# A hybrid encoder block: the seam from the first feed-forward to the mixer, and the two norms at w_out, in a new order

## The reference, cut to what matters

```python
x = x + 0.5 * swiglu(rms_norm(x, ff1_norm), ff1_w_gate, ff1_w_up, ff1_w_down)
proj = rms_norm(x, mix_norm) @ w_in                  # q | k | v | u
attn = banded_sink_attention(q, k, v, sink)          # (1024, 512)
ssm = s5_ssm_glu(u, ..., w_glu, b_glu)               # z * sigmoid(z @ w_glu + b_glu), (1024, 512)
mixed = concat(rms_norm(attn, attn_out_norm), rms_norm(ssm, ssm_out_norm))
x = x + mixed @ w_out                                # (1024, 1024)
x = x + 0.5 * swiglu(rms_norm(x, ff2_norm), ff2_w_gate, ff2_w_up, ff2_w_down)
out = rms_norm(x, final_norm)
```

## Time and profile before

| | |
|---|---|
| median of 3 runs | 1717.98 us (1716.14 to 1724.11) |
| profiled execution | 1726.49 us, span 1724.8 us, mean clock of PE 0.972 |
| PE busy | 1654.2 us, 96% |
| DVE, ACT, POOL busy | 1089.9 (63%), 726.0 (42%), 555.6 (32%) |
| longest single wait of PE | 9.05 us, before the sum at 653.84 |

### The profile page before, as it was taken

How to read it: one execution, slowest core, us unless ns; L and a number is a source line. 1 busy time by engine, 2 the same in 40 slices (tenths; PEclk the granted TensorE clock), 3 DMA queues, 4 the chain that set the end, 5 groups by cost and what they waited for, 6 DMA issues and landing times.

```text
span 1724.8 us, 21900 instructions
## 1 busy us (share of the span) xinstructions
PE 1654.2 (96%) x7540; PEld 1356.4 (79%) x7540; DVE 1089.9 (63%) x1691; ACT 726.0 (42%) x1321; POOL 555.6 (32%) x974
## 2 busy tenths in 40 slices
PE   7999999999999997999798799999999999999998
PEld 5778888888888876887576588878888888888886
DVE  5966667766778856313854536866656665667755
ACT  6444443344344435313356534444433334444443
POOL 4005788877677865100432433000000000000012
PEclk8999999999999998999788899999999999999998
DMA  6354433343795541415732025132342233685443
GB/s 210 123 91 103 135 137 125 112 136 140 249 323 169 137 133 41 157 49 105 97 67 68 25 76 175 67 98 98 102 142 99 98 115 124 228 309 164 123 110 116
DMA packets 156246, 223.23 MB, mean 129 GB/s; under 512 B 17904, under 2 KB 96368, under 8 KB 152944
## 3 DMA queue, kind: packets, MB, share of 16 engines
q1 hardware_dynamic: 153072, 214.27, 40.3%
q0 software_dynamic: 3072, 7.62, 2.3%
HBM read 151.90 MB, written 69.96 MB: 129 GB/s over the span
## 4 chain that ended last, share of the span: by engine, by line
PE 55%; POOL 24%; issue 6%; DMA 5%; DVE 5%; ACT 3%; POOLq 1%; SPq 1%; DVEq 0%; ACTq 0%
PE bank L1031 17%; PE bank L1032 16%; PE bank L1033 16%; POOL EBb L2847 2%; POOL ptmp L2846 2%; POOL ptmp L2845 2%; POOL pw L2660 2%; POOL ssq L2561 2%; POOL EBb L2861 2%; POOL ptmp L2860 2%; POOL ptmp L2859 2%; DMA cs_scratch<-EBb 1%; POOL ptmp L2806 1%; POOL ptmp L2804 1%; POOL cl_st L2810 1%
## 5 line engine op out<-in xcount | busy, mean ns | idle before, releaser
L1031 PE MATMUL bank<-hbhi,ws_lo 128*128 128x512 f32 x1056 | 414.0, 392 | 9.0 <-DVE ws_lo L2019 4.9
L1032 PE MATMUL bank<-hblo,ws_hi 128*128 128x512 f32 x1056 | 411.9, 390 | 0.0
L1033 PE MATMUL bank<-hbhi,ws_hi 128*128 128x512 f32 x1056 | 411.8, 390 | 0.0
L2561 POOL TENSOR_TENSOR ssq<-ssq,sqt 128x512 f32<-128x512 f32 x54 | 77.6, 1436 | 736.2 <-ACT sqt L1494 732.2
L1031 PE MATMUL bank<-d_hi,ws_lo 128*128 128x512 f32 x616 | 242.3, 393 | 2.2 <-DVE d_lo L2189 2.2
L1031 PEld LDWEIGHTS bank<-hbhi,ws_lo 128*128 128x128 f32 x1056 | 198.7, 188 | 56.3 <-issue 6.8
L1032 PE MATMUL bank<-d_lo,ws_hi 128*128 128x512 f32 x616 | 241.0, 391 | 0.0
L1033 PE MATMUL bank<-d_hi,ws_hi 128*128 128x512 f32 x616 | 240.9, 391 | 0.0
L1033 PEld LDWEIGHTS bank<-hbhi,ws_hi 128*128 128x128 f32 x1056 | 198.8, 188 | 41.7
L1032 PEld LDWEIGHTS bank<-hblo,ws_hi 128*128 128x128 f32 x1056 | 198.8, 188 | 41.0 <-issue 0.5
L1562 ACT ACTIVATE loc<-bank 128x512 f32<-128x512 f32 x160 | 95.6, 597 | 254.9 <-PE bank L1033 254.9
(11 more groups left out here) (273 smaller groups left out, 2656.2 us busy)
## 6 DMA issues: line engine op xcount, KB each, us to landing
b_scratch<-loc SPq DMA_DIRECT2D x42, 1024.0 KB, 7.2
d_in<-b_scratch SPq DMA_DIRECT2D x154, 256.0 KB, 3.1
raw2a<-in_ff_w_up_dram SPq DMA_DIRECT2D x44, 512.0 KB, 4.7
loc<-in_ff_w_gate_dram SPq DMA_DIRECT2D x36, 512.0 KB, 4.7
x_scratch<-xT SPq DMA_DIRECT2D x4, 2048.0 KB, 10.9
dw_lo_place<-in_ff_w_down_dram SPq DMA_DIRECT2D x8, 1024.0 KB, 7.8
xT<-x_scratch SPq DMA_DIRECT2D x8, 1024.0 KB, 6.5
x_in<-in_x_dram SPq DMA_DIRECT2D x8, 512.0 KB, 7.0
```

What stands on the lines that cost most here:

```text
L1031: nc.tensor.matmul(o, wl, rh, start=first, stop=False, skip_group_check=chain)
L1032: nc.tensor.matmul(o, wh, rl, start=False, stop=False, skip_group_check=chain)
L1033: return nc.tensor.matmul(o, wh, rh, start=False, stop=last, skip_group_check=chain)
L2561: pool.tensor_tensor(ssq[:, hs(h)], ssq[:, hs(h)], sqt[:, a % 2, :], ALU.add).then_inc(ssq_done, 1)
```

## The change

- **Seam.** `N_TAIL` is 2. Squares 0 to 3 of half 0 (tiles complete after product 1) are made on ACT before the splits of steps 40, 41, 42 and 46, and DVE adds them (`early_add`); POOL keeps four additions of half 0. For N_MIX, `ssq` and `sqt` lie in `dw_hi_place`, so ACT's wait for the landing moves behind the scalings of half 0, and POOL waits for a landing at the start of the next round. ACT's squares 4 to 9 alternate with the splits of steps 70 to 72; the Newton step of half 0 moves ahead of split 73 on DVE. The spread comes after step j = 4.
- **The end** gets the same early squares and `N_TAIL`.
- **w_out.** Halves 1 of N_ATT and N_SSM get bank 3, their own root and Newton buffers and their own diagonal; the state-space squares get `ssq_y`, `sqt_y` and semaphores of their own and go with the gates, in the order tile by tile, half 0 and half 1. Both attention sums stand behind gate 3, both spreads behind gate 5. First parts go in the order 0 to 5, both state-space sums after part 1, both spreads after part 3. Then channel tile 4 of all six blocks, tile 5 of all six, and tiles 6 and 7 block by block. Gate product 3 uses bank 4.

```diff
-N_TAIL = 3
+N_TAIL = 2
+EARLY_SQUARES = {40: 0, 41: 1, 42: 2, 46: 3}
+EARLY_ADDS = {40: 1, 41: 2, 44: 3}
...
-         + [("S", N_ATT, 6), ("S", N_ATT, 7), ("G", 2), ("R", N_ATT, 0), ("G", 3), ("G", 4)]
+         + [("S", N_ATT, 6), ("S", N_ATT, 7), ("G", 2), ("S", N_SSM, 0), ("G", 3), ("R", N_ATT, 0), ("R", N_ATT, 1)]
...
+GLU_BANK = [0, 1, 2, 4]
-SPREAD_BANK = {(N_FF2, 1): 6, (N_END, 1): 0}
+SPREAD_BANK = {(N_ATT, 1): 3, (N_SSM, 1): 3, (N_FF2, 1): 6, (N_END, 1): 0}
...
+    if norm == N_SSM:
+        return i % 2, i // 2
...
-                elif (what, n) == ("step", 5):
+                elif (what, n) == ("step", 4):
                     norm_spread(norm, 0)
...
-                    wait_lo(pe, split_before(N_FF2))
+                    wait_lo(pe, split_before(N_SSM) + 2 * (k - 3))
...
         for o in range(8):
             glu(o)
-            if o == 2 or o == 6:
-                norm_sum(N_ATT, o // 6)
-            elif o == 4 or o == 7:
-                norm_spread(N_ATT, o // 7)
-
-        pe.wait_ge(o_taken, 8)
-        out_part(0, range(4))
-        norm_sum(N_SSM, 0)
-        out_part(1, range(4))
-        norm_spread(N_SSM, 0)
-        out_part(3, range(4))
-        norm_sum(N_SSM, 1)
-        out_part(4, range(4))
-        norm_spread(N_SSM, 1)
-        out_part(2, range(4))
-        out_part(5, range(4))
+            if o == 3:
+                norm_sum(N_ATT, 0)
+                norm_sum(N_ATT, 1)
+            elif o == 5:
+                norm_spread(N_ATT, 0)
+                norm_spread(N_ATT, 1)
+
+        for i in range(6):
+            out_part(i, range(4))
+            if i == 1:
+                norm_sum(N_SSM, 0)
+                norm_sum(N_SSM, 1)
+            elif i == 3:
+                norm_spread(N_SSM, 0)
+                norm_spread(N_SSM, 1)
+        for k in (4, 5):
+            for i in range(6):
+                out_part(i, (k,))
...
-                out_part(i, range(4, KD)).then_inc(mix_out, 1)
+                out_part(i, (6, 7)).then_inc(mix_out, 1)
...
+            pool.wait_ge(eb_stored, i * 32 + 16)
...
-            pool.wait_ge(eb_stored, i * 32 + 32)
```

More of the change, by code:

```diff
@@ L87, in squares_before @@
 def squares_before(norm):
-    return sum(2 * t for t in NORM_TILES[1:norm])
+    return sum(2 * NORM_TILES[n] for n in range(1, norm) if n != N_SSM)
 def adds_before(norm):
-    return sum(2 * (t - 1) for t in NORM_TILES[1:norm])
+    return sum(2 * (NORM_TILES[n] - 1) for n in range(1, norm) if n != N_SSM)
 def sums_before(norm):
@@ L547, in htmp, with dgt, ssq_of, sqt_of @@
         return htmps[norm >= N_ATT][:, c % HTMP, :]
-    def dgt(norm):
-        return dgts[norm]
+    def dgt(norm, h):
+        return dgts[(N_ATT, N_SSM)[h]] if norm in (N_ATT, N_SSM) else dgts[norm]
+    def ssq_of(norm, h):
+        if norm == N_SSM:
+            return ssq_y[:, hs(h)]
+        return dw_hi_place[:, h, HALF:] if norm == N_MIX else ssq[:, hs(h)]
+    def sqt_of(norm, a):
+        return dw_hi_place[:, 2 + a % 2, HALF:] if norm == N_MIX else sqt[:, a % 2, :]
     def spread_bank(norm, h):
@@ L1038, in norm_sum @@
             last = max(i for i in range(2 * kt) if half_and_tile(norm, i)[0] == h)
-            pe.wait_ge(ssq_done, add_number(norm, last) + 1)
+            if norm == N_SSM:
+                pe.wait_ge(ssq_y_done, 6)
+            else:
+                pe.wait_ge(ssq_done, add_number(norm, last) + 1)
             if norm in NORMED:
-                before = split_before(norm) + h * kt
+                before = {(N_MIX, 1): KD, (N_ATT, 0): split_before(N_ATT), (N_SSM, 0): split_before(N_ATT) + 4,
+                          (N_SSM, 1): split_before(N_SSM)}.get((norm, h))
                 if before:
@@ L1487, in square @@
                     act.wait_ge(sum_ready, sums_before(norm))
-                dst = ssq[:, hs(h)]
+                dst = ssq_of(norm, h)
             else:
@@ L1688, in ffn @@
                 down_b(w, q)
-            down_split(w, range(N_SLOT, 70))
+            for q in range(N_SLOT, 70):
+                if q in EARLY_SQUARES:
+                    if (w, q) == (0, 40):
+                        act.wait_ge(t_stored, 16 * N_PAIR)
+                    down_square(w, EARLY_SQUARES[q])
+                down_split(w, (q,))
         def x_squares(h):
@@ L1877, in _ @@
             else:
-                h, k = at_[1] // 4, at_[1] % 4
-                act.wait_ge(glu_done, 2 * k + h + 1)
-                square(*at_, yT[:, k, hs(h)])
+                i = at_[1]
+                h, k = scale_order(N_SSM, i)
+                act.wait_ge(glu_done, i + 1)
+                if i >= 4:
+                    act.wait_ge(ssq_y_done, i - 3)
+                act.activation(ssq_y[:, hs(h)] if i < 2 else sqt_y[:, i % 2, :], yT[:, k, hs(h)], ACT.Square
+                               ).then_inc(sq_y_done, 1)
         def mix_src(i):
@@ L1914, in _ @@
         ffn(1)
-        for i in range(8):
-            down_square(1, i)
-        down_split(1, (70, 71, 72))
-        for i in range(8, 12):
-            down_square(1, i)
+        down_square(1, 4)
+        down_square(1, 5)
+        down_split(1, (70,))
+        down_square(1, 6)
+        down_square(1, 7)
+        down_split(1, (71,))
+        down_square(1, 8)
+        down_square(1, 9)
+        down_split(1, (72,))
         norm_std(N_END, 0)
+        down_square(1, 10)
+        down_square(1, 11)
         down_split(1, range(73, N_DSTEP))
@@ L2340, in _ @@
         ffn(0)
-        for q in range(70, 74):
+        for q in range(70, 73):
             down_split(0, q)
+        norm_rms(N_MIX, 0)
+        down_split(0, 73)
         split_lo(U_IN, U_IN + 1)
-        norm_rms(N_MIX, 0)
         down_split(0, 74)
@@ L2533, in out_rows @@
                 ins.then_inc(fin_taken, 1)
-        for q in range(70, 74):
+        for q in range(70, 73):
             down_split(1, q)
         norm_rms(N_END, 0)
+        down_split(1, 73)
         for t in range(3):
@@ L2554, in add_square @@
             h, k = half_and_tile(norm, n)
-            if begins(norm, n):
+            if begins(norm, n) or norm in (N_MIX, N_END) and n < 4:
                 return
@@ L2916, in _, with add_square_y @@
             pool.tensor_copy(mark[:, :], unit[:, 0, 0, :]).then_inc(state_done, 1)
+        def add_square_y(i):
+            if i < 2:
+                return
+            h, k = scale_order(N_SSM, i)
+            pool.wait_ge(sq_y_done, i + 1)
+            if i >= 4:
+                pool.wait_ge(ssq_y_done, i - 3)
+            pool.tensor_tensor(ssq_y[:, hs(h)], ssq_y[:, hs(h)], sqt_y[:, i % 2, :], ALU.add).then_inc(ssq_y_done, 1)
         for kind, *at_ in GATED:
-            if kind == "S":
+            if kind == "S" and at_[0] == N_SSM:
+                add_square_y(at_[1])
+            elif kind == "S":
                 add_square(*at_)
```

122 lines of the change are left out of this document (76 added, 46 removed).

## The result

The changed kernel takes 1709.28 us (median of 7 executions, 1707.12 to 1710.87), the kernel before 1724.11 (7 executions, 1716.14 to 1728.04): a ratio of 0.9919, interval 0.9899 to 0.994. So it is faster, by some 14 us, and clear of noise. 1699.0 was forecast with a range up to 1708, so the forecast is wrong: the kernel lies 1.3 us above the range. Two numbers already disagree. The profiled executions differ by 18.5 us (spans 1724.8 and 1706.3), close to the forecast's 19.0; the medians differ by 14.8. And the kernel before spreads over 12 us, the changed one over 4. The three executions of before that stand ahead of the prediction (median 1717.98) are three of these seven.

What follows compares the result with a forecast made beforehand. PE, busy 96% of the span, was taken as the bound, so only its waits and slow-clock stretches could be won: 14.8 (seam) + 2.5 (w_out) + 1.7 (end) = 19.0 off 1718.0 gave 1699.0 us, range 1692 to 1708.

Steps and rivals of the forecast that it cites:

- the Sum: Whole kernel: gains of 14.8, 2.5 and 1.7 make 19.0 us, taken off the median of 1718.0, giving 1699.0.
- the seam's lower bound of 9: Seam to the mixer: least gain, 9 us, if POOL still waits for its landing (642.6) and the sum comes at 649.4.
- The prediction's own signs of being wrong: Changed profile: PE doesn't wait for `ssq_y` at w_out, or the seam still shows more than 2 us idle.
- The seam, 14.8: First feed-forward to mixer: no PE wait at the sum or on `d_lo`; 14.8 us gained, bounds 9 and 15.3.
- W_out, 2.5: Norms at w_out: old waits go, new ones of 3.3, 1.1, 8.2 and 4.0 come; 2.5 us gained net.
- Contention, 0.3: W_out: DVE's subtractions stretched while POOL adds, charged 0.3 us since POOL is mostly idle then.
- The end, 1.7: Before the last product: 3.0 us gained, POOL's last addition 1.3 later; 1.7 net, between 0 and 3.
- (a): W_out: the hand-offs of ACT and DVE are quicker, gain 10.7 there, time 1690.8 us; chance 0.10.
- (b): W_out: 17 hand-offs are slower by 0.4 each or contend, 6.8 us in all, time 1705.8; chance 0.14.
- (c): Seam: POOL still held by its landing, sum waits 4.6 us, slow matmuls (3) stay, time 1706.6; chance 0.05.
- (d): W_out's merged sum makes it slower: w_out takes 105 us, the whole 1719; chance 0.03.
- (e): Steps 40 to 46: early squares on ACT hold up loads and PE, 2 us; chance 0.04.

Runs made afterwards that it cites:

- after_again: The changed kernel run once more with no edit, beside the kernel before: 1709.85 us, ratio to before 0.9933.
- w2_early: Against the changed kernel, the split of w_out's third unit (unit 2) put ahead of the two state-space roots: 1704.85 us, ratio to before 0.9916.

## Why the prediction was wrong

**The step that failed is the base, in the Sum:** "what changes is waits, so I take it off the median". Of the 10.3 us between 1699.0 and 1709.28, 6.1 are the base and 4.2 the terms taken off it. The base, 1717.98, was the median of three executions; with four more, run beside the changed kernel, the median of before is 1724.11, and over the 27 of after_again's group 1722.47. The terms were read from one execution of 1726.5, 8.5 above that base, and the forecast never asked what the 8.5 were. The runs show a good part of it: the wait of 9 us is itself a thing that some executions have and others don't. Of the four profiles that have the seam as before, two (times 1726.5 and 1725.4) show it and two (1716.7 and 1714.7) show one of 2.6 or 2.7. To take the whole wait off a time that may not hold it counts it twice. Whether the executions of 1716.1 and 1718.0 were of the early kind is inferred from their times; they have no profiles.

Against the profiled early execution (span 1713.0) the change is worth 6.7 us and not 19.0: 6.6 up to the wait on `qT`, and the rest cancels. Against the late one it is worth 18.5, and that looks like the forecast's 19.0, but this is partly luck. The three terms measured 13.4, 0.5 and 1.6, in sum 15.5; the mixer's 2.6, in good part chance of the clock, and 0.5 ahead of the seam fill the gap.

The range failed for the same reason: the seam's lower bound of 9 was thought out for the changed kernel (POOL still held), while the one that came true lay on the side of the kernel before (the wait mostly not there). Both hints stood in what I had: the earlier trace rows show ACT released by a DMA, and three times of one kernel spread over 8 us. The prediction's own signs of being wrong couldn't show it either: all of them are rows of the changed kernel, and nearly all came as named.

**The seam, 14.8.** 13.4 in the profiled pair (38.3 to 24.9). No wait at the sum, as forecast. Of the missing 1.4, about 0.9 is the wait of 1.16 on DVE's take of output 0, which the forecast had put 0.2 behind PE: DVE does two splits of w_in's units first (2.36 us, until 668.5). The six steps behind the spread take 16.9, or 2.82 each and not 2.72; most of that is the first matmul behind the spread. Against an early execution of before the term is 6.6, as above.

**W_out, 2.5.** The waits are right, each within 0.8 and in sum 16.9 against 17.0 with the last of 0.5. The gain is 0.5 in the profiles and nothing in the medians. The term that was mis-sized is the slow matmuls: PE was to be busy 68.0 of 85.0 and is so 70 of 87. Two sums in one piece took 3.6 for the 2.7 forecast, two spreads behind them 1.3 for 1.1, and after the 8 us wait PE's granted clock was 0.63 over 16.1 us. PE's idle time went up from 13.7 to 17.2 us, 3.3 of it for the split of unit 2, which the new order didn't need to put behind the roots (w2_early).

**Contention, 0.3.** DVE's subtraction beside POOL's additions of squares took 1.09 at 946.25 and the split of unit 1 took 1.47 for 1.23: about 0.4 and 0.2, so twice the charge and still small. The Trainium skill (GPSIMD Engine Reference, Specifications) says that GpSimd contends for SBUF with VectorE instructions that have two SBUF inputs, as both of these have; the trace agrees. The wait of 8 us is not from that.

**The end, 1.7.** 3.1 gained before the `xT` wait and 1.5 lost behind it, where PE waits 1.93 for POOL's last addition instead of 0.92: 1.6. Right in this pair; against the profiled early execution the stretch before the `xT` wait is only 1.6 shorter, and the end gives nothing.

**The rivals.** (a), (b) and (c) were about hand-offs and about POOL; none describes what happened: POOL's additions didn't wait for the landing, and the hand-offs, up to POOL's last addition at w_out, came within 1.2 us of the times worked out. (d), slower by w_out, didn't come; nor did (e), as PE ends the third step of the last product at 644.3, 0.5 earlier than before. The mixer, in which nothing was changed, moved by 2.6 in the pair of profiles; no term covered that.

## What to carry to other kernels

Before a wait is put into a sum, ask what released it: one that hangs on the landing of a DMA whose issue moves from execution to execution may belong to some executions only. Where the profiled time lies several us from the median, find what makes the difference before the sum is made, and don't take three executions for a base when they spread over 8 us. Then, put independent work into a long wait: two output parts ahead of the state-space sums, with the splits they need, took w_out's stretch from 87.1 to 79.0, 4.0 of it by the split of unit 2 alone. And in an order written by hand, look for each wait whether the thing waited for stands behind something that it doesn't need: moving one entry of the list removed the 3.3 us on the third unit.

## What the runs showed that I had not expected

- The same 108 matmuls in the mixer took 12.06, 13.67 or 15.26 us at a granted clock of 1.00, 0.88 or 0.78. They stand behind a DMA wait of 0.95, 1.29 and 1.33 us in these three; in other executions it was 13.7 behind one of 1.06, and 12.1 or 13.7 behind 1.13. The length of one wait alone doesn't tell.
- In these runs the table landed at the same time whether it was issued at 634.56 or 2.6 us later: within 641.8 to 642.8 in eleven profiles, while the issues at 631.05 and 632.43 landed 6 us earlier. With a chain that hangs on it, the profiled executions of before fall into two kinds, 7 us apart at the wait on `qT`.
- The change also took much of the spread out of the kernel: 27 executions of before span 17.3 us and 12 with only w_out changed 13.9, 12 of the changed kernel 7.8.
